# A gated linear attention block in front of a convolution and attention block: the second layer's modulation dealt over q, k and v tiles

## The reference

```python
# first block: gated linear attention, chunk 64, 4 heads (dk 128, dv 256 each)
h = rmsnorm(x, norm_g) * (1 + scale) + shift            # modulation 1, from c
q, k, v, g_lr, r = split(h @ w_in)                      # 512, 512, 1024, 16, 1024 columns
log_a = log_sigmoid(g_lr @ w_alpha + b_alpha) / 16
...                                                     # chunked recurrence over 64 tokens
x = x + gate * ((rmsnorm(o) * silu(r)) @ w_out)
x = rmsnorm(x, final_g)
# second block: its modulation depends only on c_2 and c_ctx_2, not on x
mod   = silu(c_2)     @ w_mod_2 + b_mod_2               # w_mod_2 is 1024 x 3072
mod_c = silu(c_ctx_2) @ w_mod_2 + b_mod_2
u = rms_norm(x, norm_w_2) * (1 + scale) + shift         # and so on
```

## Time and profile before

| | us |
|---|---|
| median of 3 executions | 2650.35 |
| lowest and highest of them | 2646.22, 2656.89 |
| the profiled execution, its own time | 2648.54 |
| its span in the profile | 2646.5 |
| PE busy in the span | 2470.5 (93%) |
| DVE, ACT, POOL busy | 1687.6, 1008.9, 694.6 |
| block 0, q and k tiles and modulation, about | 69 to 144 |
| block 0, gate products and v tiles, about | 144 to 199 |

### The profile page before, as it was taken

The page is one execution under the profiler, slowest core; times in us unless marked ns, Lnnn a source line. Parts: engine busy times, 40 slices in busy tenths (PEclk is TensorE's granted clock), DMA queues, the critical chain, the costliest instruction groups (busy, mean ns, idle before and its releaser), DMA issues. The chain is left out here.

```text
span 2646.5 us, 33253 instructions
## 1 busy us (share of the span) xinstructions
PE 2470.5 (93%) x11265; PEld 1698.2 (64%) x11265; DVE 1687.6 (64%) x2746; ACT 1008.9 (38%) x1766; POOL 694.6 (26%) x313
## 2 busy tenths in 40 slices
PE   3898899999999998999999976999999999988997
PEld 1576677777777777777777763554555445546776
DVE  3236564654656461889997984777777777775664
ACT  4144444444345440332222123555445445451222
POOL 1233211111211100102000003677666566640000
PEclk8999999999999999999999996999999999998999
DMA  7964787388668747488767654111111110104334
GB/s 269 358 201 141 245 289 279 132 278 318 210 220 282 275 150 271 174 283 318 236 224 240 213 177 104 49 49 54 31 31 29 30 30 25 27 25 169 131 136 153
DMA packets 225145, 453.62 MB, mean 171 GB/s; under 512 B 23957, under 2 KB 82571, under 8 KB 224756
## 3 DMA queue, kind: packets, MB, share of 16 engines
q1 hardware_dynamic: 193960, 351.04, 39.3%
q10 hardware_dynamic: 31052, 100.87, 11.1%
HBM read 328.86 MB, written 109.35 MB: 166 GB/s over the span
## 5 line engine op out<-in xcount | busy, mean ns | idle before, releaser
L2121 DVE TENSOR_REDUCE att_mx<-att_bank_m 128x1 f32<-128x512 f32 (+1 forms) x640 | 365.2, 629 | 128.9 <-PE att_bank_m L1930 128.9
L2070 ACT ACTIVATE att_p_f<-att_bank_s 128x512 f32<-128x512 f32 x576 | 312.4, 599 | 284.1 <-PE att_bank_s L1971 276.0
L1915 POOL TENSOR_TENSOR att_den<-att_den,att_p_f 128x1024 f32<-128x1024 f32 x160 | 379.4, 2371 | 42.7 <-ACT att_p_f L2070 27.4
L1618 DVE SCALAR_TENSOR_TENSOR proj_conv_acc<-proj_conv_in,proj_conv_w,proj_conv_acc 128x512 f32<-128x512 f32 (+1 forms) x480 | 337.4, 772 | 0.0
L562 PE MATMUL gla_bank_g<-mid_a_hi,mid_w_hi 128*128 128x512 f32 x768 | 310.8, 405 | 2.0 <-POOL mid_w_lo L515 1.1
L562 PE MATMUL gla_bank_g<-mid_a_hi,mid_w_lo 128*128 128x512 f32 x768 | 300.8, 392 | 0.0
L562 PE MATMUL gla_bank_g<-mid_a_lo,mid_w_hi 128*128 128x512 f32 x768 | 300.1, 391 | 0.0
L1945 PE MATMUL att_bank_o<-att_p_f,att_v 128*64 128x512 f32 x1152 | 270.6, 605 | 0.0
L562 PEld LDWEIGHTS gla_bank_g<-mid_a_hi,mid_w_hi 128*128 128x128 f32 x768 | 144.9, 189 | 48.3 <-issue 18.5
L1945 PEld LDWEIGHTS att_bank_o<-att_p_f,att_v 128*64 128x64 f32 x1152 | 74.6, 137 | 146.0 <-issue 104.9
L562 PEld LDWEIGHTS gla_bank_g<-mid_a_hi,mid_w_lo 128*128 128x128 f32 x768 | 144.6, 188 | 31.5
(11 more groups left out here) (404 smaller groups left out, 4753.7 us busy)
## 6 DMA issues: line engine op xcount, KB each, us to landing
mid_w_hi<-scratch_w_hi SPq DMA_DIRECT2D x100, 512.0 KB, 4.5
mid_w_lo<-scratch_w_lo SPq DMA_DIRECT2D x100, 512.0 KB, 6.1
mid_w_hi<-scratch_w_hi ACTq DMA_DIRECT2D x84, 512.0 KB, 3.9
mid_w_lo<-scratch_w_lo ACTq DMA_DIRECT2D x84, 512.0 KB, 5.0
scratch_w_hi<-mid_w_hi SPq DMA_DIRECT2D x54, 512.0 KB, 6.3
scratch_w_lo<-mid_w_lo SPq DMA_DIRECT2D x54, 512.0 KB, 7.1
mod_wslab<-in_ada_w SPq DMA_DIRECT2D x6, 2048.0 KB, 18.4
first_w_raw<-in_gla_w_in SPq DMA_DIRECT2D x24, 512.0 KB, 6.7
```

The source lines that it names most:

```text
L1618: dve.scalar_tensor_tensor(acc, src, conv_w[:, c, k:k + 1], acc, ALU.mult, ALU.add).then_inc(taps, 1)
L1915: pool.tensor_tensor(den[s][:], pair(0) if j == 1 else den[s][:], pair(j), ALU.add).then_inc(den_pool, 1)
L2070: act.activation(p_f[:, kt, :], S[kt % SBANKS][:], ACT.Exp, scale=float(HD) ** -0.5).then_inc(p_done, 1)
L2121: dve.reduce_max(mx[:, qt, n:n + 1], M[p % MBANKS][:, 0:min(TB, KEYS - TB * n)], AX_X).then_inc(mx_read, 1)
```

## The change

Slabs 0, 1 and 2 are used after q/k tiles 1, 3 and 6 in place of all six after tiles 0 to 5, and slabs 3, 4 and 5 after v tiles 0, 2 and 4. There are now three places: slab 0 in `v_tok`, slabs 1, 3 and 5 in `o_t`, slabs 2 and 4 in `xr`. Slab 2 is loaded after q/k tile 1 without a wait, slab 3 after tile 4, slab 4 after tile 7 and slab 5 after v tile 1. `turn_row(0)` and `turn_row(1)` come after tiles 2 and 4, and `turn_row(2)` inside tile 7, ahead of its fifth slice. The late slabs go into PSUM bank `O[:, 1]` in place of `T[1]`, from the moment that ACT has copied the gate products. `turn_row` of a late slab comes after the next v tile and its `transpose_v`. DVE's part is cut in two: `copy_row` for the first three slabs and a first `add_bias` before the v tiles; then `copy_row(3)`, `(4)` and `(5)` each right behind the copy of v tile 0, 2 and 4, and the second `add_bias` with the gains behind the copy of v tile 5.

```diff
-        wslab = (v_tok[:].rearrange("p t n -> p (t n)").rearrange("p (k n) -> p k n", k=KT), o_t)
+        in_v = v_tok[:].rearrange("p t n -> p (t n)").rearrange("p (k n) -> p k n", k=KT)
+        wslab = (in_v, o_t, xr, o_t, xr, o_t)
+        EARLY = 3
+        MOD_AT = {1: 0, 3: 1, 6: 2}
+        MOD_LATE_AT = {0: 3, 2: 4, 4: 5}
...
+        def mod_bank(n):
+
+            return T[1] if n < EARLY else O[:, 1, :]
...
# PE
                 def modulate(n):
 
-                    pe.wait_ge(slab_landed[n % 2], UP + 16 * (n // 2) + 16)
+                    pe.wait_ge(slab_landed[n], UP + 16)
+                    if n == EARLY:
+                        pe.wait_ge(zc, UP + 4)
                     pe.wait_ge(row_copied, UP + GROUPS * n)
...
-                            gemm(b * 8 + g, s, between=None if not b or s else ...)
+                            gemm(b * 8 + g, s, between=(lambda: turn_row(EARLY - 1)) if b == 0 and g and s == 3 else None if not b or s else ...)
                             j = 4 * g + s
-                            if b == 0 and 1 <= j <= NS:
-                                turn_row(j - 1)
-                            if b == 0 and j < NS:
-                                modulate(j)
+                            if b == 0 and j < 7 and j - 1 in MOD_AT:
+                                turn_row(MOD_AT[j - 1])
+                            if b == 0 and j in MOD_AT:
+                                modulate(MOD_AT[j])
...
                         gemm(b * 8 + 2 + j // 4, j % 4)
                         if j:
                             transpose_v(j - 1)
+                        if b == 0 and j - 1 in MOD_LATE_AT:
+                            turn_row(MOD_LATE_AT[j - 1])
+                        if b == 0 and j in MOD_LATE_AT:
+                            modulate(MOD_LATE_AT[j])
...
                     pe.wait_ge(v_copied, UP + b * 8 + 9)
+                    if b == 0:
+                        pe.wait_ge(mod_step, UP + 4)
# ACT
-                        if b == 0 and 1 <= j < NS - 1:
-                            act.wait_ge(slab_used, UP + j)
-                            load_slab(j + 1)
+                        if b == 0 and j == 1:
+                            load_slab(2)
+                        if b == 0 and j == 4:
+                            act.wait_ge(slab_used, UP + 2)
+                            load_slab(3)
+                        if b == 0 and j == 7:
+                            act.wait_ge(slab_used, UP + 3)
+                            load_slab(4)
...
+                        if b == 0 and j == 1:
+                            act.wait_ge(slab_used, UP + 4)
+                            load_slab(5)
# DVE
-                for n in range(NS):
+                for n in range(EARLY):
                     copy_row(n)
-                dve.wait_ge(row_turned, UP + NS)
...
+                add_bias(range(EARLY))
...
                         dve.wait_ge(vt, UP + b * 8 + j + 1)
                         dve.tensor_copy(v_tok[:, :, tok(j)], ...).then_inc(v_copied, 1)
+                        if b == 0 and j in MOD_LATE_AT:
+                            copy_row(MOD_LATE_AT[j])
+                        if b == 0 and j == 5:
+                            add_bias(range(EARLY, NS))
+                            dve.wait_ge(mod_step, UP + 4)
+                            for v in range(1, 3):
+                                dve.scalar_tensor_tensor(gains[:, v, :], ...).then_inc(mod_step, 1)
```

More of the change, by code:

```diff
@@ L372, in gla_block @@
         csil, group_sum = keep["csil"], keep["group_sum"]
-        wslab = (v_tok[:].rearrange("p t n -> p (t n)").rearrange("p (k n) -> p k n", k=KT), o_t)
+        in_v = v_tok[:].rearrange("p t n -> p (t n)").rearrange("p (k n) -> p k n", k=KT)
[3 more added lines that the diff above has]
+        MOD_LATE_AT = {0: 3, 2: 4, 4: 5}
         mod_row = [on[0:GROUP_ROWS, WC * i:WC * (i + 1)] for i in range(2)]
-        mod_bank, mod_at = T[1], O[:, 0, 0:6 * KT].rearrange("p (j v) -> p j v", v=2)
-        slab_landed = [sem(f"slab_landed{i}") for i in range(2)]
+        mod_at = O[:, 0, 0:6 * KT].rearrange("p (j v) -> p j v", v=2)
+        slab_landed = [sem(f"slab_landed{i}") for i in range(NS)]
+        def mod_bank(n):
+            return T[1] if n < EARLY else O[:, 1, :]
         rows_clear, slab_used, row_copied, row_turned, mod_step = (
@@ L584, in modulate @@
                         g = k % GROUPS
-                        last = pe.matmul(mod_bank[GROUP_GAP * g:GROUP_GAP * g + 2, :], csil[:].rearrange("p (v k) -> p k v", k=KT)[:, k, 1:3],
-                                         wslab[n % 2][:, k, :], start=(k < GROUPS), stop=(k >= KT - GROUPS))
+                        last = pe.matmul(mod_bank(n)[GROUP_GAP * g:GROUP_GAP * g + 2, :], csil[:].rearrange("p (v k) -> p k v", k=KT)[:, k, 1:3],
+                                         wslab[n][:, k, :], start=(k < GROUPS), stop=(k >= KT - GROUPS))
                     last.then_inc(slab_used, 1)
@@ L669, in _ @@
                                 pe.wait_ge(x1, UP + b * 8 - 1 + s)
-                            gemm(b * 8 + g, s, between=None if not b or s else (lambda: sum_squares(b - 1)) if g == 0 else (lambda: sum_squares_of_h(b - 1)))
+                            gemm(b * 8 + g, s, between=(lambda: turn_row(EARLY - 1)) if b == 0 and g and s == 3 else None if not b or s else (lambda: sum_squares(b - 1)) if g == 0 else (lambda: sum_squares_of_h(b - 1)))
                             j = 4 * g + s
-                            if b == 0 and 1 <= j <= NS:
-                                turn_row(j - 1)
-                            if b == 0 and j < NS:
-                                modulate(j)
+                            if b == 0 and j < 7 and j - 1 in MOD_AT:
+                                turn_row(MOD_AT[j - 1])
+                            if b == 0 and j in MOD_AT:
+                                modulate(MOD_AT[j])
                     pe.wait_ge(glr_copied, UP + b + 1)
@@ L792, in load_slab @@
                 def load_slab(n):
-                    act.dma_start(wslab[n % 2][:] if n % 2 else wslab[0], d["w_mod_2"].rearrange("(k p) n -> p k n", p=P)[:, :, WC * n:WC * (n + 1)]
-                                  ).then_inc(slab_landed[n % 2], 16)
+                    act.dma_start(wslab[n][:, :, :], d["w_mod_2"].rearrange("(k p) n -> p k n", p=P)[:, :, WC * n:WC * (n + 1)]
+                                  ).then_inc(slab_landed[n], 16)
                 for n in range(2):
@@ L1007, in copy_row, with add_bias @@
                         part = slice(GROUP_GAP * g, GROUP_GAP * g + 2)
-                        dve.tensor_copy(mod_row[n % 2][part, :], mod_bank[part, :]).then_inc(row_copied, 1)
-                for n in range(NS):
-                    copy_row(n)
-                dve.wait_ge(row_turned, UP + NS)
[L1012 to L1017, removed]
+                        dve.tensor_copy(mod_row[n % 2][part, :], mod_bank(n)[part, :]).then_inc(row_copied, 1)
+                def add_bias(slabs):
+                    part = slice(slabs.start * (WC // P), slabs.stop * (WC // P))
+                    dve.wait_ge(row_turned, UP + slabs.stop)
+                    for v in range(1, 3):
+                        dve.tensor_tensor(modv[:, v, part], mod_at[:, part, v - 1], col("b_mod_2")[:, part], ALU.add).then_inc(mod_step, 1)
+                for n in range(EARLY):
+                    copy_row(n)
+                add_bias(range(EARLY))
                 for b in range(0, NB):
@@ L1026, in _ @@
                         dve.tensor_copy(v_tok[:, :, tok(j)], T[j % 2][:].rearrange("p (t i) -> p t i", t=NT)).then_inc(v_copied, 1)
+                        if b == 0 and j in MOD_LATE_AT:
[3 more added lines that the diff above has]
+                            dve.wait_ge(mod_step, UP + 4)
+                            for v in range(1, 3):
+                                dve.scalar_tensor_tensor(gains[:, v, :], modv[:, v, 8:16], 1.0, col("norm_w_2"), ALU.add, ALU.mult).then_inc(mod_step, 1)
                         if j == 2:
```

## The result

The changed kernel takes 2657.02 us (median of 12), the kernel before 2651.8 us (median of 12 beside it): ratio 1.0024, 95% interval 1.0013 to 1.0035. That is 5.2 us slower, a real difference but under half a per cent. Forecast were 2655 us and +4.75 us.

A forecast was written before the change was run, and what follows sets the result against it. PE, busy 2470.5 of 2646.5 us, was taken to bound the kernel. The terms -13.45 + 2.55 + 11.7 + 5.4 - 1.45 = +4.75 us on 2650.35 gave 2655 us, range 2644 to 2664.

The forecast's parts named there:

- slab waits and slow clock removed: q/k tiles: PE's three slab waits (9.6 us) and the slow clock after long ones (3.85 us) go: -13.45 us.
- new waits in the q/k tiles: PE gets ahead of weights at tiles 2 (1.75 us) and 4 (0.6), and waits at `turn_row(2)` (0.2): +2.55 us.
- three stalls on DVE's row copies: v tiles: PE waits at each late `turn_row` for DVE's v copy and four row copies, 3.9 us each: +11.7 us.
- slow clock behind them: v tiles: PE's clock falls after each of three idle times, 1.8 us each: +5.4 us, bounds 0 and 7.
- waits absorbed: v tiles: PE arrives later, so waits for weights of 1.09 and about 0.35 us go: -1.45 us.
- Tile 2's wait (a): q/k tile 2: PE arrives at 82.2, before its weights are ready at 83.95, and waits 1.75 us.
- Tile 4's wait (b): q/k tile 4: PE arrives before its weights are ready and waits 0.6 us, between 0.1 and 0.9.
- the clock stays up: Rival, v tiles: the stalls come but PE's clock does not fall; sum -0.65 us, so 2650; chance 0.2.
- the weights' chain binds on a large scale: Rival, closer packed tiles: raw weight loads landing after 16.5 us set the pace; 14 us more, 2669; chance 0.1.
- No slab was late: Judges the rival that a slab is still late, by 2 to 4 us, giving 2658; chance 0.05.

The follow-up runs named there:

- experiment 3: The changed kernel with each late slab's four row copies made as one copy of 98 partitions; ratio to the kernel before 0.9988.
- experiment 7: The changed kernel with DVE's row copies of slabs 3, 4 and 5 ahead of the v copy, PE's order unchanged; ratio to the kernel before 0.9984.
- experiment 1: The changed kernel with the turns of slabs 3, 4 and 5 one v tile later; 2641.44 us, ratio to the kernel before 0.9960.
- experiment 4: The changed kernel with slabs 2 to 5 loaded only in their first eighth; ratio to the kernel before 1.0021.
- experiment 6: The changed kernel with late turns one v tile later, slab 2 used after q/k tile 5 and turned after tile 6; ratio to the kernel before 0.9961.
- experiment 2: The changed kernel with 13 unused matmuls ahead of each late turn, keeping PE busy while it waits; ratio to the kernel before 1.0003.
- experiment 8: The kernel before with three slab places, slab 2 issued after q tile 0 and not at the start; ratio to the kernel before 0.9971.
- experiment 5: The kernel before with a third slab place only, slabs 0 to 2 issued at the start; 2643.83 us, ratio to the kernel before 0.9972.

## Why the prediction was right

By its own steps, in the profiled executions:

| term of the sum, us | forecast | measured |
|---|---|---|
| slab waits and slow clock removed | -13.45 | -13.45 (both gone) |
| new waits in the q/k tiles | +2.55 | about +1.1 (0.94 at tile 4, 0.17 at `turn_row(2)`) |
| three stalls on DVE's row copies | +11.7 | +11.35 (3 x (148.08 - 143.94 - 0.36)) |
| slow clock behind them | +5.4 | +5.8 |
| slow clock in the gate products | 0 | +1.6 |
| waits absorbed | -1.45 | -1.45 |
| sum | +4.75 | about +5.0 |

The stretches themselves give +5.1, the medians +5.2.

**The stalls** came three times, at the place and of the size that the order of PE and DVE gave; experiments 3 and 7 show that they hang on the row copies, experiment 1 that nothing else stood behind them. **The clock** term was right in sum. Its reasoning, that the length of idle time with the turn beside it decides, was not: two stalls of 1.38 us had the same effect. The forecast took its price from two falls of the kernel before, and that happened to serve. **Tile 2's wait (a)** of 1.75 us did not come in this execution, because PE's first tile began 2.5 us later than before while the raw load landed at 80.61, only 0.3 us later than before (80.31). What counts is how far the load lands behind the first tile's start. That was 11.0 us in the kernel before, on which the forecast rests, and 8.8 us in this execution. In experiments 4, 6 and 7 it was 10.2 to 10.4 us, and there the wait came, with 1.10, 1.03 and 0.97 us. So the term was over-sized, and it varies from run to run. **Tile 4's wait (b)** was forecast at 0.6 and came as 0.94 us. **The gate products** are a term that I didn't have: 125.65 to the next slab's product at 136.54 is 10.9 us, against 133.31 - 124.01 = 9.3 us in experiment 6, where the clock stayed up. It about cancelled the missing wait (a). So the total is closer to the measurement than its parts are, and that is luck.

**The rivals.** That the clock stays up was refuted, and experiment 2 shows what it would have given: 1.0003. That the weights' chain binds on a large scale was refuted for this change by its own trace, with 0.9 us of such waits, and by experiment 4. Raw loads as slow as the prediction feared (16.5 us) came only near in experiment 8, with a median of 15.5 us for three, and cost 4.0 us of waits there. No slab was late in any kernel with three places. The third place alone is worth 7 to 8 us in the timed runs, which the prediction didn't consider: I had taken the removed waits as the gain of dealing out, and they are mostly the gain of the place.

The better versions are experiments 1 and 6, both 0.996 of the time before. Both keep the change. The first only moves the three late turns, the other also moves slab 2's product and turn.

## What to carry to other kernels

When work of a second engine is moved along with its consumer, look at what now stands between the two on both queues. Here the producer waits for an instruction that stands just ahead of the consumer, so a handover that was free became a stall of 3.5 us, three times, and each gave back half as much again in slow clock. Place the consumer one step later than the data, not right behind its trigger. And before spreading loads out, try one more buffer: here it removed the same waits with a few lines. It is also worth looking at when its load is issued, for a third issue at the start held ACT (3.37 us).

## What was unexpected of the hardware

- The clock fell to the 1.2 GHz level without PE idle just before, in the gate products (contraction over 32 rows) behind half a tile and a turn of tiny matmuls (129 to 132 us of the changed kernel, at 0.50). It also fell behind two of three stalls of only 1.38 us in experiment 3, whereas it stayed up behind 1.98 us in the kernel before.
- The third 2 MB DMA issued in a row on ACT's queue took 3.37 us to issue, against 0.41 and 0.60 for the first two and 0.37 to 0.41 for later ones issued one at a time (experiment 5).
